# Value products of the latent-attention layer once per head pair over four query tiles, with modulation slots and output weights placed elsewhere

## What is computed

```python
def mla_attend(q_nope, q_pe, keys, w_uk, w_uv, w_o):
    q_lat = jnp.einsum('bthn,chn->bthc', q_nope, w_uk)
    q = jnp.concatenate([q_lat, q_pe], axis=-1)[:, :, None]
    o = block_attention(q, keys[:, :, None, :], keys[:, :, None, :KV_LORA], MLA_SCALE)[:, :, 0]
    o = jnp.einsum('bthc,chv->bthv', o, w_uv).reshape(B, T, MLA_HEADS * MLA_V)
    return o @ w_o
# per layer: mod = silu(c) @ ada_w[l] + ada_b[l], split into six shift, scale and gate vectors
# context queries read 128 context keys; latent queries read 640 keys (128 cached, 512 latent)
# softmax over all keys of a query, then x = x + gate * mix, then the experts
```

## Time and profile before

| | us |
|---|---|
| median of three runs | 1293.39 (1291.4 to 1294.76) |
| profiled execution | 1292.7 |
| its span, first to last instruction | 1290.9 |
| PE busy in the span | 1231.8 (95%) |
| one pair of attention 1, from a query product to the next pair's same one | 32.33 |

### The profile page before, as it was taken

The page is one execution under the profiler, slowest core; times in us unless marked ns, Lnnn a source line. Parts: engine busy times, 40 slices in busy tenths (PEclk is TensorE's granted clock), DMA queues, the critical chain, the costliest instruction groups (busy, mean ns, idle before and its releaser), DMA issues.

```text
span 1290.9 us, 17251 instructions
## 1 busy us (share of the span) xinstructions
PE 1231.8 (95%) x5561; PEld 681.9 (53%) x5562; DVE 589.3 (46%) x1338; ACT 409.8 (32%) x855; POOL 58.2 (5%) x63
## 2 busy tenths in 40 slices
PE   7999999999999999998978999799999999999997
PEld 4554566666664475443434444466654574444443
DVE  1322455555552574322228544888735663322216
ACT  2332344444451121111022325677732111111122
POOL 0103000000000020000002000000000110000002
PEclk9999999999999999999998999899999999999999
DMA  9979999622244057999987000600020279999947
GB/s 373 414 312 407 414 413 410 259 100 100 100 186 165 33 202 244 355 355 356 364 313 267 9 1 9 256 1 1 2 99 0 102 274 317 355 293 334 352 183 265
DMA packets 88357, 290.18 MB, mean 225 GB/s; under 512 B 9209, under 2 KB 27580, under 8 KB 86876
## 3 DMA queue, kind: packets, MB, share of 16 engines
q1 hardware_dynamic: 46032, 185.68, 39.4%
q0 software_dynamic: 16640, 64.59, 12.7%
q10 hardware_dynamic: 25612, 38.96, 8.9%
HBM read 214.48 MB, written 74.73 MB: 224 GB/s over the span
## 4 chain that ended last, share of the span: by engine, by line
PE 80%; DMA 6%; DVE 5%; ACT 3%; SPq 3%; issue 2%; ACTq 1%; DVEq 1%; POOL 0%; POOLq 0%
PE ps L2114 16%; PE ps L1724 11%; PE ps L1741 10%; PE ps L2143 7%; PE ps L1666 7%; PE ps L1994 6%; PE ps L1957 4%; PE ps L1769 3%; PE ps L2193 3%; PE ps L1818 3%; PE ps L1686 2%; DMA arena<-in_moe_gu 2%; PE ps L2056 2%; PE ps L1950 2%; PE ps L1967 2%
## 5 line engine op out<-in xcount | busy, mean ns | idle before, releaser
L2114 PE MATMUL ps<-arena 128*128 (+1 forms) x560 | 247.7, 595 | 0.0
L2114 PEld LDWEIGHTS ps<-arena 128*128 128x128 f32 x560 | 104.5, 191 | 118.1 <-issue 118.0
L1666 PE MATMUL ps<-const,arena 128*128 128x128 f32 (+2 forms) x1000 | 145.4, 279 | 18.0 <-DMA const<-in_const 8.2
L1724 PE MATMUL ps<-arena 128*128 128x512 f32 (+2 forms) x400 | 152.1, 535 | 4.6 <-DVE arena L1246 1.2
L1666 PEld LDWEIGHTS ps<-const,arena 128*128 128x128 f32 (+2 forms) x1000 | 115.8, 142 | 76.6 <-issue 39.8
L1139 DVE TENSOR_REDUCE hst<-ps 128x1 f32<-128x640 f32 (+1 forms) x160 | 110.9, 714 | 94.0 <-PE ps L1994 80.1
L1741 PE MATMUL ps<-arena 128*128 128x512 f32 x320 | 142.0, 597 | 1.4 <-issue 1.4
L2143 PE MATMUL ps<-arena 128*128 (+1 forms) x280 | 126.1, 593 | 2.2 <-ACT arena L844 2.2
L721 ACT ACTIVATE arena<-ps,hst 128x640 f32<-128x640 f32 (+1 forms) x160 | 112.4, 706 | 42.0 <-DVE hst L1139 42.0
L1724 PEld LDWEIGHTS ps<-arena 128*128 128x128 f32 x400 | 74.4, 190 | 74.1 <-issue 58.1
L1741 PEld LDWEIGHTS ps<-arena 128*128 128x128 f32 x320 | 59.1, 190 | 69.8 <-issue 69.7
(11 more groups left out here) (218 smaller groups left out, 1173.9 us busy)
## 6 DMA issues: line engine op xcount, KB each, us to landing
arena<-in_moe_gu SPq DMA_DIRECT2D x128, 512.0 KB, 13.1
arena<-in_ada_w SPq DMA_DIRECT2D x62, 768.0 KB, 11.9
slot_rows<-arena POOLq DMA_DIRECT2D x10, 4096.0 KB, 67.7
arena<-in_moe_w_down SPq DMA_DIRECT2D x64, 512.0 KB, 16.1
slot_rows<-arena ACTq DMA_DIRECT2D x33, 512.0 KB, 8.5
arena<-slot_rows ACTq DMA_DIRECT2D x124, 128.0 KB, 13.4
arena<-mod_rows SPq DMA_DIRECT2D x12, 512.0 KB, 12.3
arena<-in_gqa_w_qkv SPq DMA_DIRECT2D x12, 512.0 KB, 13.7
```

The costliest lines, as they stand in the source:

```text
L1666: return nc.tensor.transpose(out, in_, ident[0:rows, 0:rows])
L1724: last = mm(bank(2 + b, cols), hT[l](t)[:, k * P:(k + 1) * P], w[:, k], start=k == 0, stop=k == KD - 1)
L2114: last = mm(bank(gu_bank(u)), e_xsT[:, nth(u, D)][:, k * P:(k + 1) * P], w(k * BANK, BANK), start=k == 0, stop=k == KD - 1)
```

## The change

The ten products of 128 columns for each latent tile become ten products of 512 columns for the four latent tiles of a pair together, in two parts: key blocks 0 to 2 at r = 2 of the next pair and 3 to 4 at r = 3 (`LATENTS_AT`). The context tile's stays at r = 4 (`prompt`). For the pair's probabilities to lie side by side, ACT's copy writes each key block with a gap, into one of two arrays of 5 x 512 columns (`M_PT`, one for each head of the pair). The second array lies where modulation slot 0 was, and a small one for the context (`M_PP`) behind it. So layer 1's modulation weights use slots 2 and 1 in place of 0 and 1, `w_wo0` is loaded after the last piece that used slot 2, and the first experts' loads wait until the last value product is done.

```diff
+LATENTS_AT = ((2, 0, 3), (3, 3, NB))
-    PT = ar(18560, 4 * LKEYS)
+    M_PT, M_PP = (ar(18560, NB * BANK), ring(10240, NB * BANK)), ring(12800, 2 * P)
-        return ADA_SLOT[j] if j < ADA_0 else (j - ADA_0) % 2
+        return ADA_SLOT[j] if j < ADA_0 else 2 - (j - ADA_0) % 2
...
         def experts(l):
+            if l == 0:
+                sp.wait_ge(S("pv_done"), PV0)
             load_gu(l, 0)
...
-        sp.wait_ge(S("ada_made"), ADA_0 - 2)
-        load(S("wo_landed", 0), w_wo0, A["mla_w_o"][0], KD)
         for j in range(ADA_0, ADA_ALL):
             load_ada(j)
...
+        sp.wait_ge(S("ada_made"), 1 + max(j for j in range(ADA_ALL) if ada_slot_of(j) == 2))
+        load(S("wo_landed", 0), w_wo0, A["mla_w_o"][0], KD)
         sp.wait_ge(S("made"), len(MAKES) * PAIR)
         load(S("wo_landed", 0), w_wo1, A["mla_w_o"][1], KD)
...
-                    if j >= 4:
-                        act.wait_ge(S("pv_done"), (j - 4) // 2 + 1)
-                    act.activation(ptbuf(j, keys), ps[:, 4 * BANK:4 * BANK + keys], ACT.Copy).then_inc(S("pt_ready"), 1)
+                    if m:
+                        act.wait_ge(S("pv_done"), latent_done(m - 1) if it else prompt_done(m - 1))
+                    turned = ps[:, 4 * BANK:4 * BANK + keys]
+                    act.activation(pt_out_m(j), split(turned, NB) if it else turned, ACT.Copy).then_inc(S("pt_ready"), 1)
...
+            def latents(m, first, end):
+                if first == 0:
+                    pe.wait_ge(S("pt_ready"), (m + 1) * PER_PAIR)
+                    if m:
+                        pe.wait_ge(S("oT_latent"), m)
+                for j in range(first, end):
                     for odd in range(2):
+                        last = mm(bank(6)[VD * odd:VD * (odd + 1)], v_of(2 * m + odd, j), M_PT[odd][:, j * BANK:(j + 1) * BANK],
+                                  start=j == 0, stop=j == NB - 1)
+                if end == NB:
+                    last.then_inc(S("pv_done"), 1)
...
-                if s >= 4 and s % 2 == 0:
-                    pair((s - 4) // 2)
+                m, r = divmod(s, PER_PAIR)
+                if m < PAIR and r == PROMPT_AT:
+                    prompt(m)
+                for at, first, end in LATENTS_AT:
+                    if m and r == at:
+                        latents(m - 1, first, end)
```

More of the change, by code:

```diff
@@ L326, in turned_at, with pt_out_m @@
         return 4 * BANK if s % 2 == 0 else 6 * BANK if keys == P else 6 * BANK - P
-    def ptbuf(s, n):
-        return PT[:, (s % 4) * LKEYS:(s % 4) * LKEYS + n]
+    def pt_out_m(s):
+        m, it, h, keys = step(s)
+        if it == 0:
+            return M_PP[:, (h % 2) * P:(h % 2 + 1) * P]
+        return split(M_PT[h % 2], NB)[:, :, (it - 1) * P:it * P]
     def pt_out_g(s):
@@ L337, in pt_out_g, with prompt_done, latent_done @@
         return split(W_PT[half][h % 2], NB)[:, :, at * P:(at + 1) * P]
-    PV0 = PAIR * NTILE
+    PV0 = 2 * PAIR
     CTX, HALF = 1, (2, 3)
+    def prompt_done(m):
+        return 2 * m + 1
+    def latent_done(m):
+        return 2 * m + 2
     def wide_done(m, part):
@@ L363, in half_bank @@
         return bank(7, QW, half * QW)
-    def oT_out(it):
-        return bank(7, P) if it == 0 else bank(6, P, (it - 1) * P)
     def oT_block(l, m, it, n=1):
@@ L728, in heads @@
                     j = s - 2
-                    keys = step(j)[3]
+                    m, it, _, keys = step(j)
                     act.wait_ge(S("p_turned"), j + 1)
-                    if j >= 4:
-                        act.wait_ge(S("pv_done"), (j - 4) // 2 + 1)
-                    act.activation(ptbuf(j, keys), ps[:, 4 * BANK:4 * BANK + keys], ACT.Copy).then_inc(S("pt_ready"), 1)
+                    if m:
+                        act.wait_ge(S("pv_done"), latent_done(m - 1) if it else prompt_done(m - 1))
+                    turned = ps[:, 4 * BANK:4 * BANK + keys]
+                    act.activation(pt_out_m(j), split(turned, NB) if it else turned, ACT.Copy).then_inc(S("pt_ready"), 1)
                 if s < STEPS:
@@ L1120, in prompt_out @@
         def prompt_out(l, m):
-            dve.wait_ge(S("pv_done"), wide_done(m, CTX) if l else m * NTILE + 1)
+            dve.wait_ge(S("pv_done"), wide_done(m, CTX) if l else prompt_done(m))
             nc.vector.tensor_copy(oT_block(l, m, 0), bank(7, P)).then_inc(S("oT_prompt"), 1)
         def latent_out(m):
-            dve.wait_ge(S("pv_done"), m * NTILE + NTILE)
+            dve.wait_ge(S("pv_done"), latent_done(m))
             nc.vector.tensor_copy(oT_block(0, m, 1, LAT), bank(6)).then_inc(S("oT_latent"), 1)
@@ L1756, in heads, with prompt @@
         def heads(score, v_of, hook):
-            def pair(p):
-                m, it = divmod(p, NTILE)
-                blocks, first = (1, 5) if it == 0 else (LKEYS // P, 0)
-                pe.wait_ge(S("pt_ready"), 2 * p + 2)
-                if it == 0:
-                    spare_free(m, PROMPT_AT)
-                if m and it == 1:
-                    pe.wait_ge(S("oT_latent"), m)
-                for j in range(blocks):
+            def prompt(m):
+                pe.wait_ge(S("pt_ready"), m * PER_PAIR + 2)
+                spare_free(m, PROMPT_AT)
+                for odd in range(2):
+                    last = mm(bank(7, P)[VD * odd:VD * (odd + 1)], v_of(2 * m + odd, NKEYT - 1), M_PP[:, odd * P:(odd + 1) * P],
+                              start=True, stop=True)
+                last.then_inc(S("pv_done"), 1)
[5 more added lines that the diff above has]
+                for j in range(first, end):
                     for odd in range(2):
-                        last = mm(oT_out(it)[VD * odd:VD * (odd + 1)], v_of(2 * m + odd, first + j),
-                                  ptbuf(2 * p + odd, blocks * P)[:, j * P:(j + 1) * P], start=j == 0, stop=j == blocks - 1)
-                last.then_inc(S("pv_done"), 1)
+                        last = mm(bank(6)[VD * odd:VD * (odd + 1)], v_of(2 * m + odd, j), M_PT[odd][:, j * BANK:(j + 1) * BANK],
+                                  start=j == 0, stop=j == NB - 1)
+                if end == NB:
+                    last.then_inc(S("pv_done"), 1)
             for s in range(STEPS + 4):
```

## The result

The changed kernel takes 1297.98 us in the median (1295.95 to 1301.86), the kernel before beside it 1291.37: a ratio of 1.0047, interval 1.0035 to 1.0059. The forecast of 1290.9 was wrong in size and in sign. The profiled execution after has a span of 1294.1 us against 1290.9.

What follows compares the result with a forecast made beforehand. PE's list was taken to bound attention 1's middle pairs (32.33 us). Pair 0 -2.9, pairs 1 to 6 -3.0, pair 7 +0.2 and tail +3.2 gave -2.5 us: forecast median 1290.9 us, range 1288.0 to 1294.5.

Steps and rivals of the forecast that it cites:

- Wide products: Attention 1's value products: parts of 2.74 and 1.88 us replace four narrow blocks, 0.74 us less in a pair.
- The rival drawn from the Trainium skill: Value products: two array halves at 512 columns reach only 1.59 times, 1299.7 us in all; halves not streaming together got 0.05.
- A price for each pass: Rival: each pass costs 25 ns, so 60 fewer in a pair save 12 us in all, 1279 us; chance 0.01.
- The wait at r = 1: Pairs 1 to 6: a turning waits 0.24 us for ACT's copy, leaving 0.50 of the 0.74 us gain.
- Pair 0, pair 7 and the tail: Attention 1's ends: pair 0 loses 2.9 us, pair 7 gains 0.2, the uncovered last block adds 3.2.
- Moved transfers: Later loads of output weights and first experts' weights, costed at nothing.
- The rival of late parts: Output projection: modulation parts land up to 5.2 us later behind expert transfers, 1291.5 to 1296.1 us; chance 0.12.
- The early gain: Rival near 90 us: output weights leave full queues, PE's 1.19 us wait shrinks, 1288.3 to 1289.7 us; chance 0.14.

Runs made afterwards that it cites:

- e9: Changed kernel with the last pair's latent products split in two parts and SP instead of ACT issuing layer 1's modulation transfers: 1287.22 us, ratio 0.9958.
- e3: Changed kernel with ACT issuing the two transfers of a modulation product one turn later: 1291.92 us, ratio 1.0006.
- e10: Changed kernel with POOL's zeroing of the table held back until pair 0's latent products are done: 1296.96 us.
- e6: Kernel before with 64 empty instructions at the start of PE's program: 1297.21 us, ratio 1.0037.
- e2: Kernel before with only the moved transfers, value products staying narrow: 1291.62 us, ratio 1.0.
- e5: Changed kernel with 39 empty instructions at the start of PE's program: 1293.82 us, ratio 1.0011.
- e14: Changed kernel with 60 empty instructions at the start of PE's program: 1294.65 us, ratio 1.0015.
- e12: Changed kernel with 246 empty instructions at the start of PE's program: 1325.82 us.

## Why the prediction was wrong

**Wide products: right.** 2.74 and 1.88 us were forecast, 2.73 and 1.87 measured; a pair without waits takes 31.70 us (e9), 0.63 less than 32.33, where 0.74 was forecast. So the seams are real, and two halves at 512 columns stream together: four passes more cost 0.86 us, 0.215 each, where the output projection's 32 passes of 512 columns over the whole width of the array take 13.97, 0.44 each. The rival drawn from the Trainium skill (TensorE: Matmul & The Clock Gate, Measured speedup vs the span model), by which two halves would fall short of twice the speed, is out: as an estimate by that page 1.59 times would have made these passes longer by a quarter. A price for each pass is out as well.

**The wait at r = 1: this term was mis-sized.** The step read ACT's issue in pair 7 (1.02 us) and used it for pairs 1 to 6. In pairs 1 to 3 it is 1.8, since POOL's zeroing fills the queues until about 241 us, and their turnings of r = 0 and 1 stand 3.04 to 3.08 us apart. So those pairs got longer by 0.34 us in place of shorter by 0.50: 3 x 0.84 = 2.5 us, as much as the whole forecast gain. Where the issue lasts 1.0 the step was right: pairs 4 and 5 came out at -0.42 and -0.47 for -0.50, and the turnings of r = 0 and 1 stand 2.31 us apart for 2.30. e3 and e10 show the cause.

**Pair 0, pair 7 and the tail: right, part by part.** Up to the first key product of pair 1, pair 0 lost 2.89 us for -2.9. From r = 0 of pair 6 on, -0.5 + 0.2 + 3.2 = +2.9 was forecast, and +2.99 measured (61.93 to 64.92). The wait of 1.35 at r = 1 of pair 7 only takes the place of the block: from the turning at r = 0 it is 2.30 us before and 2.28 after, 0 as forecast. The 1.84 ahead of the last turning are the 0.60 of before and the block of 1.24 that stood there: from the turning ahead of it to the last one it is 2.61 us in both traces (380.89 to 383.50 after; 388.24 before, from the row below). Between these places pair 7 got 0.23 longer for +0.2, and from the last turning to the projection it is +3.19 (3.69 to 6.88) for +3.2. Attention 1 as a whole came to +0.24 for -2.5, and the r = 1 term makes up nearly all of that.

```profile
385.63 0.77 PE L1666 MATMUL ps<-const,arena 128*128 128x128 f32 x5
```

**Moved transfers: right.** No wait for the output weights, and the modulation parts came no later. The wait of 0.45 went, -0.51, but it went in e6 too, where no transfer moved. The rival of late parts is out (after, e2).

**What the prediction never had: the stages behind were carried over unchanged.** Its sum gave them nothing, without a reason, and they hold the loss. A change that removes 960 instructions from PE moves each later refill; the gathers of two stages happened to stand clear of them before and stand behind them now. In the profiled run that is 0.61 + 0.68 + 2.9 = 4.2 us of the table. The 0.68 belongs to it: from layer 1's first projection to the final gathers the seven profiles with a transfer just ahead of these take 566.2 to 567.3 us, the ten others 565.4 to 565.8. The +0.70 is not shown to be the transfers'. e6 puts 5.1 us on the kernel before (1297.21 against 1292.12 beside it). e5 takes 4.2 and e14 3.3 off the changed kernel.

**The rest of the median's 6.6 us** is not settled in full. The table's rows behind the start of attention 1 add up to +5.1, which leaves 1.5. The profiled run of after is the fastest of its six (1295.95) and has no fall of the clock at 105 us or in the tail; the falls in the uncovered tail, 1.5 to 2.9 us each in three of eight profiles, are likely a part of what its other runs take more. The early gain, a rival with 0.14, showed in the profile (-1.79) but is the clock's chance and not the change's.

## What to carry to other kernels

A change in the number of PE's instructions moved all its later refills here, so a difference of some microseconds in code that was not touched is to be looked for among the instruction transfers first, and a few empty instructions at the start of the program test it (246 were too many: they cost 27 us). What an issue or a wait costs is to be read at the place where it will stand, with queues as full as there. Where products are gathered into larger ones, the last group has nothing beside it: split it, and keep small ones for the end.

## What the runs showed of the hardware

One transfer of 16.4 KB, 0.96 us on one of sixteen engines, made the end 1.6 to 4.9 us longer when it came 1.3 to 1.6 us ahead of the first gather. Between 1256 and 1266 us the median gather takes 6.3 us to land before and 8.3 after, and the final norm's weights 5.5 and 7.7:

```profile
arena<-in_final_norm ACTq DMA_DIRECT2D x1, 512.0 KB, 5.5
slot_rows<-arena ACTq DMA_DIRECT2D x1, 256.0 KB, 4.3
arena<-slot_rows,slot_i POOLq DMA_INDIRECT x6, 6.3
```

```profile
arena<-in_final_norm ACTq DMA_DIRECT2D x1, 512.0 KB, 7.7
slot_rows<-arena ACTq DMA_DIRECT2D x1, 256.0 KB, 2.2
arena<-slot_rows,slot_i POOLq DMA_INDIRECT x4, 8.3
```

So the gathers and the weights land about 2 us later, while the one store of 256 KB issued there lands 2 us sooner. Why a packet of 1 us holds the former up by twice its own length, no view of the profile tells. An empty instruction of PE at the program's start took about 0.16 us, as an estimate from e12 (246 in the 38.66 us up to PE's first product). Granted clocks of 0.50 followed PE's waits of 1.2 and 1.84 us in some runs and not in others of the same program.
